# Norms summed by token, the queries' rotation packed, and the gated-attention stage's filling matmuls moved one unit earlier

## The chip, the cores and the metric

One core of a Trainium2 chip runs the whole program. The metric is the device time of one execution in microseconds, the median of the runs shown. The engines are named as in the profile: PE is TensorE, DVE is VectorE, ACT is ScalarE, POOL is GpSimd, SP is SyncE.

## The reference, cut to what matters

A transformer block (multi-head latent attention "MLA", gated linear attention "GLA", a merge, a convolutional feed-forward) is followed by four layers of another kind. Only the first block's token mixer is touched. All is float32, 512 latent tokens and 256 context tokens, 768 together.

```
q = heads(rms_norm(q_c, q_norm_g) @ w_uq)              # 8 heads of 64 + 32 (the 32 are rotated)
k_nope, v = heads(rms_norm(kv_c, kv_norm_g) @ w_ukv)   # 8 heads
p = softmax((q_nope k_nope + rope(q_rope) rope(k_rope)) * MLA_SCALE)
# GLA: 4 heads, 2 directions, chunks of 64 tokens
b_cum = cumsum(g) in the chunk;  kd = k * exp(b_last - b_cum);  ke = k * exp(-b_cum);  qe = q * exp(b_cum)
decay = exp(b_last);  state' = decay * state + kd^T v;  o = mask(qe ke^T) v + qe state
y = rms_norm(o, norm_g) * silu(r)                       # per token and head, over 128 channels
```

## The kernel before

Activations lie channels on partitions, tokens along the free axis. A product in high precision is three fp32r matmuls (high*high, high*low, low*high). `project` makes one output of 128 channels x 512 tokens from k-tiles of a weight panel, `both` makes two outputs (512 latent and 256 context tokens) from the same tiles, `mm` is the line L1576. SP streams weight panels, POOL splits each into `w_hi` and `w_lo`.

Outputs are numbered in one sequence and go to four banks of `acc` in turn: output n may begin only when output n-4 has been taken (`begin_out`, `out_taken`). `both` waits for both of its banks before its first matmul. Every engine works through its own list strictly in order.

The GLA stage is eight units u (head u//2, direction u%2), in the order that `gla_order()` gives. In a unit PE does `turned` (six transposes of the decayed keys kd, L641), `intra` (scores within chunks, L647), `added` (what each chunk adds to the state, L662 and L667), in units 2, 4 and 6 `sum` (L672: the squared outputs of the head before, summed over channels by a matmul with ones, which gives 512 columns on all 128 partitions), `gate` of unit u+2 (L632), a filling projection from `GLA_FILL` (k, q or r of a later head), and the unit's `gla_output` (L684, L690). DVE does `decays(u+1)` (zb, a scan to b_cum, the differences b_last - b_cum into kd, L1244 and L1245), `masked_scores(u)`, `states(u)` (a copy and seven steps, L1292), `decayed_keys(u+1)`, `decayed_queries(u+1)`, and the head's normalisation `head_output` with a reciprocal over 512 columns (L1265). ACT takes outputs from the banks (L868), and makes the exponentials (`key_decays` L934, `sum_decays`, `gate_logs`), squares and roots.

The queries' and keys' low-rank norms are applied by DVE to z_q and z_kv (`low_rank_queries`, `low_rank_keys`) inside units 0 and 1. After the GLA stage PE projects eight outputs for the queries (one a head: 64 plain rows, 32 rotary rows and their 32 partners), then the last head's `sum`, four `both` for the keys, and six value outputs. DVE turns the rotary rows head by head (three operations of 32 partitions each), copies k_rope to the heads, and finishes the last GLA head. Then come 32 attention units of scores, `exps` (L1016), `normalised`, `turn_probs` (L735) and `values` (L752).

Of the kernel before, what the change touches and what calls it, by code (L numbers as in the profile page):

```python
# [70 lines left out]
GH = 4  # L71
# [34 lines left out]
GLA_FILL = [("k", 1, 2), ("q", 1, 1), ("k", 2, 2), ("q", 2, 1), ("k", 3, 2), ("q", 3, 1), ("r", 2, 1), ("r", 3, 1)]  # L106


def gla_order():
    order = [("gate", 0, 2), ("k", 0, 2), ("gate", 1, 2)]  # L110
    for u in range(GLA_STEPS):
        order += [("turned", u, 2), ("intra", u, 1), ("added", u, 1)]
        if u % 2 == 0 and u:
            order.append(("sum", u // 2 - 1, 1))
        if u + 2 < GLA_STEPS:
            order.append(("gate", u + 2, 2))
        order.append(GLA_FILL[u])
    return order
# [5 lines left out]
OUT_V = OUT_KH + HEADS  # L124
# [51 lines left out]
def build(nc, io, names, upto=None, start_x=False):  # L176

    n_panels = io["weights"].shape[0]
    with ExitStack() as whole:
# [163 lines left out]
        with ExitStack() as first:  # L343
# [9 lines left out]
            fb("fill_first", [P, LINE // 8])  # L353
# [5 lines left out]
            with ExitStack() as part:  # L359
# [31 lines left out]
                decay_w = fa("decay_w", [P, GH * P])  # L391
                intra_mask = fa("intra_mask", [P, 2, P])
# [3 lines left out]
                chunk_decay = fa("chunk_decay", [P, 2, NCH])  # L396
            with ExitStack() as part:
# [36 lines left out]
        o_norm = square_sum  # L434

# [25 lines left out]
        gla_d = sem("gla_d")  # L461
# [10 lines left out]
        lr_scaled = sem("lr_scaled")  # L472
        lr_hi = sem("lr_hi")
        lr_lo = sem("lr_lo")
        q_copied = sem("q_copied")
# [73 lines left out]
        def first_block_pe(pe, turn, next_tile, mm, begin_out, project, tile, norm_sum, skip_to_panel):  # L549
# [55 lines left out]
            out = begin_out()  # L605
            for k in range(QL):
                ins = pe.matmul(out[:, :], ones[:, :], low_square[:, T * k:T * k + T], start=(k == 0), stop=(k == QL - 1))
            ins.then_inc(out_made, 1)
            for c0, c1 in ((0, T), (T, TC)):
                out = begin_out()  # L610
                for k in range(KVL):
                    at = QL * T + TC * k
                    ins = pe.matmul(out[:, 0:c1 - c0], ones[:, :], low_square[:, at + c0:at + c1], start=(k == 0),
                                    stop=(k == KVL - 1))
                ins.then_inc(out_made, 1)

            def gla_part(name, i):
# [76 lines left out]
            for name, i, _ in gla_order():  # L694
                gla_part(name, i)
                if (name, i) in [part[:2] for part in GLA_FILL]:
                    gla_output([part[:2] for part in GLA_FILL].index((name, i)))
# [6 lines left out]
            for pair in range(HEADS // 2):  # L704
                both([(kv_hi[:, k, 0:T], kv_lo[:, k, 0:T]) for k in range(KVL)],
                     [(kv_hi[:, k, T:TC], kv_lo[:, k, T:TC]) for k in range(KVL)], T, C,
                     (lambda k: pe.wait_ge(lr_lo, QL + k + 1)) if pair == 0 else None)
            slot, _ = next_tile()
# [99 lines left out]
        def first_block_act(act, feed):  # L808
# [105 lines left out]
            take(OUT_QNORM, square_sum[:, :], func=ACT.Sqrt, bias=col("eps"), scale=1.0 / (QL * P))  # L914
            take(OUT_KVNORM, square[:, 0, :], func=ACT.Sqrt, bias=col("eps"), scale=1.0 / (KVL * P))
            take(OUT_KVNORM + 1, square[:, 1, 0:C], func=ACT.Sqrt, bias=col("eps"), scale=1.0 / (KVL * P), width=C)
# [32 lines left out]
            def head_square(h):  # L949
                act.wait_ge(gla_o, 2 * h + 2)  # L950
                if h == 0:
                    act.wait_ge(lr_scaled, 1)
                act.activation(square[:, h % 2, :], side[:, h % 2, :], ACT.Square).then_inc(gla_sq, 1)

            def head_root(h):
                if h:
                    act.wait_ge(gla_y, h)
                take(OUT_GLA["sum", h], root[:, :], func=ACT.Sqrt, bias=col("eps"), scale=1.0 / P)
                load_exp_ln()

# [8 lines left out]
            gate_logs(1)  # L969
            for u in range(GLA_STEPS):  # L970
# [1504 lines left out]
```

## Time and profile before

| | |
|---|---|
| Median of 3 runs | 3150.24 us (3149.42 to 3150.46) |
| The profiled execution | 3147.42 us, span 3145.4 us |
| PE, POOL, DVE, ACT busy | 97%, 66%, 46%, 22% of the span |
| The chain that ended last | PE 90%, DVE 7%, ACT 2% |

How to read it: PE sets the time, and the rest of the kernel follows it. So the sum of what PE waits, and of what it does at a low granted clock, is what can be won or lost. In windows, PEclk is the mean granted clock as a share of full speed; the two levels are 1.2 and 2.4 GHz. In a timeline, a bracket behind a row is the time for which the engine stood idle ahead of it, and what released it.

### The profile page before, as it was taken

Reading aid. Unit: us, or ns where it says so; the run is one execution under the profiler, and the core shown is the slowest. Engines: PE = TensorE matmul, PEld = TensorE weight load, DVE = VectorE, ACT = ScalarE, POOL = GpSimd, SP = SyncE. Lnnn points to the kernel's source line nnn. Section 1 sums busy time; section 2 is a strip of 40 time slices with the busy share of each in tenths; the row PEclk is TensorE's granted clock in tenths of the full one; section 3 lists DMA queues with packets and bytes.
Section 4 is the critical chain, followed back from the end, with each engine's and each line's share of the span. In section 5 each row is a group of like instructions: output and inputs, shape, how many; then the busy total and the mean of one; then the engine's idle time right before and its main releaser. Section 6 shows DMA issues by size and latency. Waiting matters only on the chain.

```text
span 3145.4 us, 38638 instructions
## 1 busy us (share of the span) xinstructions
PE 3038.9 (97%) x13632; PEld 2471.6 (79%) x13632; DVE 1431.6 (46%) x1871; ACT 681.5 (22%) x1187; POOL 2066.3 (66%) x2056
## 2 busy tenths in 40 slices
PE   5889999999999999999999999999999999999998
PEld 3767668778887788888888888888888887888886
DVE  7877852276456664222325322255422246542222
ACT  3244651111002542111122111100211115421110
POOL 4622217666666677777767777777777776777774
PEclk8989999999999999999999999999999999999999
DMA  6611112222222232232322222222222322332221
GB/s 257 246 41 37 34 54 94 94 81 99 96 97 91 94 102 99 94 100 94 107 87 90 98 94 100 94 97 97 94 100 94 100 94 94 101 100 95 97 97 67
DMA packets 86026, 306.73 MB, mean 98 GB/s; under 512 B 9552, under 2 KB 10064, under 8 KB 85648
## 3 DMA queue, kind: packets, MB, share of 16 engines
q1 hardware_dynamic: 82512, 297.73, 28.0%
q10 hardware_dynamic: 3392, 7.28, 0.7%
q8 instruction: 88, 1.44, 0.2%
q14 instruction: 34, 0.28, 0.0%
HBM read 302.87 MB, written 2.10 MB: 97 GB/s over the span
## 4 chain that ended last, share of the span: by engine, by line
PE 90%; DVE 7%; ACT 2%; issue 1%; SPq 1%; DMA 1%; DVEq 0%; ACTq 0%
PE acc L1576 85%; PE acc L725 1%; DVE rec_rec_x L1999 1%; PE side L752 1%; DVE ada_more L1152 1%; DMA xc<-in_ctx 1%; SPq L531 1%; PE side L735 0%; PE side L1576 0%; PE acc L647 0%; PE stat L1639 0%; DVE n_scaled L1129 0%; PE acc L632 0%; DVE rec_rec_x L1997 0%; DVE att_stat L1347 0%
## 5 line engine op out<-in xcount | busy, mean ns | idle before, releaser
L1538 POOL TENSOR_TENSOR w_lo<-w_raw,w_hi 128x512 fp32r<-128x512 f32 x513 | 671.8, 1310 | 1011.2 <-PE acc L1576 982.9
L1576 PE MATMUL acc<-h_hi,w_hi 128*128 128x512 f32 x2224 | 876.2, 394 | 28.7 <-ACT gq L868 11.6
L1576 PE MATMUL acc<-h_lo,w_hi 128*128 128x512 f32 x2224 | 868.5, 391 | 0.0
L1576 PE MATMUL acc<-h_hi,w_lo 128*128 128x512 f32 x2224 | 868.4, 390 | 0.0
L1539 POOL TENSOR_TENSOR w_lo<-w_raw,w_hi 128x512 fp32r<-128x512 f32 x513 | 709.4, 1383 | 0.0
L1576 PEld LDWEIGHTS acc<-h_hi,w_hi 128*128 128x128 f32 x2224 | 418.9, 188 | 130.2 <-issue 16.8
L1576 PEld LDWEIGHTS acc<-h_lo,w_hi 128*128 128x128 f32 x2224 | 419.5, 189 | 85.5 <-issue 1.9
L1576 PEld LDWEIGHTS acc<-h_hi,w_lo 128*128 128x128 f32 x2224 | 419.4, 189 | 85.2
L1527 POOL TENSOR_SCALAR w_hi<-w_raw 128x512 fp32r<-128x512 f32 x513 | 403.7, 787 | 37.1 <-DMA w_raw<-in_weights 37.1
L1968 DVE TENSOR_TENSOR x<-acc,x 128x512 f32 (+1 forms) x160 | 110.7, 692 | 661.8 <-PE acc L1576 661.7
L1576 PE MATMUL acc<-mlp_hid_hi,w_hi 128*128 128x512 f32 x1024 | 398.3, 389 | 0.0
L1576 PE MATMUL acc<-mlp_hid_lo,w_hi 128*128 128x512 f32 x1024 | 398.3, 389 | 0.0
L1576 PE MATMUL acc<-mlp_hid_hi,w_lo 128*128 128x512 f32 x1024 | 398.3, 389 | 0.0
L1528 POOL TENSOR_SCALAR w_hi<-w_raw 128x512 fp32r<-128x512 f32 x513 | 338.5, 660 | 0.0
L1896 ACT ACTIVATE mlp_hidden<-mlp_relu 128x512 f32<-128x512 f32 x128 | 81.1, 633 | 880.5 <-DVE mlp_relu L2198 880.5
L1975 DVE TENSOR_TENSOR mlp_hid_lo<-mlp_hidden,mlp_hid_hi 128x512 f32 (+1 forms) x128 | 172.3, 1346 | 177.3 <-ACT mlp_hid_hi L1897 177.3
L1576 PEld LDWEIGHTS acc<-mlp_hid_lo,w_hi 128*128 128x128 f32 x1024 | 192.2, 188 | 40.0
L1576 PEld LDWEIGHTS acc<-mlp_hid_hi,w_hi 128*128 128x128 f32 x1024 | 192.2, 188 | 39.9
L1576 PEld LDWEIGHTS acc<-mlp_hid_hi,w_lo 128*128 128x128 f32 x1024 | 192.2, 188 | 39.8
L2198 DVE SCALAR_TENSOR_TENSOR mlp_relu<-acc,norms 128x512 f32<-128x512 f32 x128 | 88.5, 692 | 255.1 <-PE acc L1576 254.5
L1758 ACT ACTIVATE side<-x 128x512 f32<-128x512 f32 x64 | 38.6, 603 | 454.6 <-DVE x L1968 454.6
L1424 DVE SCALAR_TENSOR_TENSOR ff_conv<-acc,table,ff_conv 128x441 f32<-128x441 f32 (+2 forms) x176 | 122.4, 695 | 6.3
(347 smaller groups left out, 3543.4 us busy)
## 6 DMA issues: line engine op xcount, KB each, us to landing
w_raw<-in_weights SPq DMA_DIRECT2D x513, 512.0 KB, 3.3
ada<-in_ada SPq DMA_DIRECT2D x36, 512.0 KB, 5.7
ada_more<-in_ada SPq DMA_DIRECT2D x10, 512.0 KB, 18.2
x<-in_x ACTq DMA_DIRECT2D x16, 256.0 KB, 6.6
out<-x SPq DMA_DIRECT2D x8, 256.0 KB, 2.2
cvec<-in_cvec ACTq DMA_DIRECT2D x1, 1024.0 KB, 5.8
ada_n<-in_ada SPq DMA_DIRECT2D x2, 512.0 KB, 17.3
xc<-in_ctx SPq DMA_DIRECT2D x1, 1024.0 KB, 16.7
```

Of the source, the lines that this page charges most:

```text
L531: sp.dma_start(ada_slot[slot], io["ada"][m]).then_inc(ada_in[slot], 16)
L1424: ins = dve.scalar_tensor_tensor(out=out, in0=src[:, r0 + r:r1 + r, c0 + c:c1 + c], scalar=col("conv_w", FF1 * tap + j), in1=out, op0=ALU. ...
L1527: pool.tensor_scalar(w_hi[:, slot, 0:half], w_raw[:, slot, 0:half], 1.0, 1.0, ALU.mult, ALU.mult)
L1528: pool.tensor_scalar(w_hi[:, slot, half:], w_raw[:, slot, half:], 1.0, 1.0, ALU.mult, ALU.mult).then_inc(hi_made, 1)
L1538: pool.tensor_tensor(w_lo[:, slot, 0:half], w_raw[:, slot, 0:half], w_hi[:, slot, 0:half].bitcast(F32), ALU.subtract)
L1539: pool.tensor_tensor(w_lo[:, slot, half:], w_raw[:, slot, half:], w_hi[:, slot, half:].bitcast(F32), ALU.subtract).then_inc(panel_made, 1)
L1576: ins = pe.matmul(out, lhs, rhs, start=start, stop=stop, skip_group_check=group)
L1758: act.activation(squares(norm, k), x[:, k, :], ACT.Square).then_inc(squared, 1)
L1896: act.activation(M["hidden"][:, o % 4, :], M["relu"][:, o % 4, :], ACT.Square)
L1968: dve.tensor_tensor(tile, bank(o), tile, ALU.add).then_inc(out_taken[o % BANKS], 1)
L1975: dve.tensor_tensor(lo, whole_, hi.bitcast(F32), ALU.subtract).then_inc(made_sem, 1)
L2198: dve.scalar_tensor_tensor(out=M["relu"][:, o % 4, :], in0=bank(o), scalar=0.0, in1=rstd[:, :], op0=ALU.max, op1=ALU.mult).then_inc(out_ta ...
```

## The change

- `k` of head 1 is projected ahead of unit 0; the fillings of units 0 to 4 are then q1, k2, q2, k3, q3, unit 5 has none, and units 6 and 7 keep r2 and r3.
- The differences on DVE (L1244, L1245) go. `key_decays` on ACT copies the chunks' last sums (two small operations), and makes kd by nine exponentials, eight of 64 columns and one of 256, each with the last sum as its bias.
- Sums of squares go by token: the squares are the stationary operand and one column of ones the moving one, so a sum is one column for each block of 128 tokens. Roots and reciprocals are of 4 to 10 columns. A new part `spread` gives a head's factor back to all partitions: ACT makes a diagonal (four copies of the identity scaled by a factor), PE multiplies it by ones, DVE reads the result from the bank in `head_output`. `spread` of a head stands one unit behind its `sum`. `keys` does the same for z_kv (six copies, two matmuls).
- The queries' low-rank factor is not applied to z_q: it goes into the scale of the softmax (`score_scale`, a column operand of `exps` and of the negated maximum), and the channel gain q_norm into `zq_hi` and `zq_lo`.
- The queries' outputs are packed: outputs 0 to 3 hold the rotary rows and partners of four heads each, outputs 4 to 7 the plain rows of two heads each. DVE turns four heads in three operations of 128 partitions, ACT and DVE copy the result to the heads. `rope_q` (512 KB) is loaded by a DMA on ACT's queue behind unit 7.

```diff
-GLA_FILL = [("k", 1, 2), ("q", 1, 1), ("k", 2, 2), ("q", 2, 1), ("k", 3, 2), ("q", 3, 1), ("r", 2, 1), ("r", 3, 1)]
+GLA_FILL = [("q", 1, 1), ("k", 2, 2), ("q", 2, 1), ("k", 3, 2), ("q", 3, 1), None, ("r", 2, 1), ("r", 3, 1)]
-    order = [("gate", 0, 2), ("k", 0, 2), ("gate", 1, 2)]
+    order = [("gate", 0, 2), ("k", 0, 2), ("gate", 1, 2), ("k", 1, 2)]
...
+        if u % 2 == 1 and u > 1:
+            order.append(("spread", u // 2 - 1, 1))
+        if u == GLA_STEPS - 1:
+            order.append(("keys", 0, 2))
...
                 if name == "sum":
-                    pe.matmul(out[:, :], ones[:, :], square[:, i % 2, :], start=True, stop=True).then_inc(out_made, 1)
+                    for b in range(4):
+                        ins = pe.matmul(out[:, b:b + 1], square[:, i % 2, P * b:P * b + P], ones[:, 0:1], start=True, stop=True)
+                    ins.then_inc(out_made, 1)
+                if name == "spread":
+                    pe.wait_ge(head_diag, i + 1)
+                    out = begin_out()
+                    pe.matmul(out[:, :], ones[:, :], square[:, i % 2, :], start=True, stop=True).then_inc(out_made, 1)
...
             def key_decays(u):
-                act.wait_ge(gla_d, u + 1)
-                act.activation(kd[:, :], kd[:, :], ACT.Exp, scale=1.0 / GATE_NORM).then_inc(gla_ed, 1)
+                act.wait_ge(gla_b, u + 1)
+                act.activation(sums_[:, 0:NCH], b_cum[:, last], ACT.Copy, scale=1.0 / GATE_NORM)
+                link(act.activation(sums_[:, NCH:NCH + 1], b_cum[:, end:end + 1], ACT.Copy, scale=1.0 / GATE_NORM))
+                for n in range(NCH + 1):
+                    cols = slice(CHUNK * n, CHUNK * n + CHUNK) if n < NCH else slice(T, TC)
+                    ins = act.activation(kd[:, cols], b_cum[:, cols], ACT.Exp, scale=-1.0 / GATE_NORM, bias=sums_[:, n:n + 1])
+                ins.then_inc(gla_ed, 1)
...
+            def head_diagonal(h):
+                act.wait_ge(head_inverse, h + 1)
+                for b in range(4):
+                    ins = act.activation(square[:, h % 2, P * b:P * b + P], identity[:, :], ACT.Copy, scale=head_rstd[:, 1, b:b + 1])
+                ins.then_inc(head_diag, 1)
+            def key_diagonal():
+                act.wait_ge(low_inverse, 1)
+                for b in range(KB):
+                    ins = act.activation(key_spread[:, P * b:P * b + P], identity[:, :], ACT.Copy, scale=low_rstd[:, 4 + b:5 + b])
+                ins.then_inc(key_diag, 1)
...
-                gla_take(*GLA_FILL[u][:2])
+                if GLA_FILL[u]:
+                    gla_take(*GLA_FILL[u][:2])
+                if d == 0 and h:
+                    head_diagonal(h - 1)
+                if u == GLA_STEPS - 2:
+                    key_diagonal()
+                    for k in range(QL):
+                        act.activation(zq_hi[k], z_q[:, k, :], ACT.Copy, scale=col("q_norm", k)).then_inc(lr_hi, 1)
...
+            head_diagonal(GH - 1)
             for tb in range(KB):
                 take(OUT_V + tb, v_mla[:, tb, :])
...
-                    act.activation(prob[:, u % 2, c0:c1], bank(o + i)[:, 0:c1 - c0], ACT.Exp, scale=MLA_SCALE,
+                    act.activation(prob[:, u % 2, c0:c1], bank(o + i)[:, 0:c1 - c0], ACT.Exp, scale=score_scale[:, 0, qb:qb + 1],
...
             def head_output(h):
-                wait_taken(dve, OUT_GLA["sum", h])
-                link(dve.reciprocal(root[:, :], root[:, :]))
...
+                o = OUT_GLA["spread", h]
+                take(dve.scalar_tensor_tensor(out=o_norm[:, :], in0=gr[:, h % 2, :], scalar=col("gla_norm"),
+                                              in1=bank(o), op0=ALU.mult, op1=ALU.mult), o)
+                own(dve.tensor_tensor(o_norm[:, :], side[:, h % 2, :], o_norm[:, :], ALU.mult), gla_y, h + 1)
...
-                dve.tensor_scalar(kd[:, T:TC], b_cum[:, T:TC], b_cum[:, end:end + 1], -1.0, ALU.subtract, ALU.mult)
-                own(dve.tensor_tensor(chunks(kd[:, 0:T]), chunks(b_cum[:, 0:T])[:, :, last_of[d]].to_broadcast([P, NCH, CHUNK]),
-                                      chunks(b_cum[:, 0:T]), ALU.subtract), gla_d, u + 1)
...
                 if u + 1 < GLA_STEPS:
                     decayed_keys(u + 1)
                     decayed_queries(u + 1)
+                if d == 0 and h:
+                    head_inverses(h - 1)
+                if d == 1 and h:
                     head_output(h - 1)
```

The order of PE at the end of `added` in unit 4 of before, where head 1's sum (`norms,ones`), the gates (`glow,decay_w`) and the filling k of head 3 (`h_hi,w_hi`) follow:

```order
L667 MATMUL side<-v_tok,kd_tok 128x128
L667 MATMUL stat<-v_tok,kd_tok 128x128
L672 MATMUL acc<-norms,ones 128x512 [waits out_taken0,gla_sq]
L632 MATMUL acc<-glow,decay_w 128x512 [waits out_taken1]
L632 MATMUL acc<-glow,decay_w 128x256 [waits out_taken2]
L1576 MATMUL acc<-h_hi,w_hi 128x512 [waits panel_made,out_taken0,out_taken3]
L1576 MATMUL acc<-h_lo,w_hi 128x512
```

And of the change at the end of `added` in unit 3, where the same k of head 3 now follows head 0's spread (`norms,ones`) and the gates:

```order
L686 MATMUL stat<-v_tok,kd_tok 128x128
L686 MATMUL side<-v_tok,kd_tok 128x128
L697 MATMUL acc<-norms,ones 128x512 [waits out_taken2,head_diag]
L651 MATMUL acc<-glow,decay_w 128x512 [waits out_taken3]
L651 MATMUL acc<-glow,decay_w 128x256 [waits out_taken0]
L1649 MATMUL acc<-h_hi,w_hi 128x512 [waits panel_made,out_taken2,out_taken1]
L1649 MATMUL acc<-h_lo,w_hi 128x512
```

The filling has moved a unit ahead, and the output four ahead of its second bank is now the spread and no longer the sum.

The order of DVE in unit 4 of before, from the keys of unit 5 (kd) and queries (`ada`, ke) on to the normalisation of head 1:

```order
L1253 TENSOR_TENSOR kd<-kd,gk 128x768 [waits out_taken0,gla_ed,out_taken3,gla_s]
L1259 TENSOR_TENSOR ada<-ada,gq 128x512 [waits out_taken3,gla_e,gla_kd]
L1260 TENSOR_TENSOR ke<-ke,gk 128x512 [waits dve_chain]
L1265 RECIPROCAL norms<-norms 128x512 [waits out_taken0,gla_qk]
L1268 SCALAR_TENSOR_TENSOR norms<-side,table,norms 128x512 [waits gla_o,out_taken1,dve_chain]
L1270 TENSOR_TENSOR norms<-norms,gr 128x512 [waits dve_chain]
L1232 SCALAR_TENSOR_TENSOR zb<-acc,ln 128x512 [waits gla_ln,gla_y]
```

And of the change in unit 3, from the keys of unit 4 on; `norms<-gr,table,acc` is the operation that reads the spread's bank:

```order
L1309 TENSOR_TENSOR kd<-kd,gk 128x768 [waits out_taken1,gla_ed,out_taken0,gla_s]
L1315 TENSOR_TENSOR qe<-qe,gq 128x512 [waits out_taken1,gla_e,gla_kd]
L1316 TENSOR_TENSOR ke<-ke,gk 128x512 [waits dve_chain]
L1332 SCALAR_TENSOR_TENSOR norms<-gr,table,acc 128x512 [waits out_made,out_taken0,gla_qk]
L1334 TENSOR_TENSOR norms<-side,norms 128x512 [waits out_taken2]
L1295 SCALAR_TENSOR_TENSOR zb<-acc,ln 128x512 [waits gla_ln,gla_y]
L1297 SCALAR_TENSOR_TENSOR zb<-acc,ln 128x256 [waits out_taken3]
```

The reciprocal is gone from the row, and the operation that empties the spread's bank stands behind the multiplications for the next unit.

The order of ACT in unit 6 of the change, from head 2's root on; `gr` is the filling r2, `norms<-identity` are the two diagonals, `hc_hi` and `hc_lo` are zq_hi, `kd_tok` are the takes of unit 7's `turned`:

```order
L901 ACT_TABLE_LOAD
L901 ACTIVATE head_rstd<-acc,table 128x4 [waits out_made]
L844 ACT_TABLE_LOAD
L901 ACT_TABLE_LOAD [waits out_made]
L901 ACTIVATE gr<-acc 128x512 [waits gla_y]
L1004 ACTIVATE norms<-identity,head_rstd 128x128 [waits head_inverse]
L1004 ACTIVATE norms<-identity,head_rstd 128x128 x3
L1010 ACTIVATE norms<-identity,low_rstd 128x128 [waits low_inverse]
L1010 ACTIVATE norms<-identity,low_rstd 128x128 x5
L1044 ACTIVATE hc_hi<-x,table 128x512
L1044 ACTIVATE hc_lo<-x,table 128x512 x2
L901 ACTIVATE kd_tok<-acc 128x512 [waits out_made]
L901 ACTIVATE kd_tok<-acc 128x256 [waits out_made]
```

Ten copies have come in between the take of r2 and the takes of unit 7's transposes.

## Rows read from the trace of the kernel before

**Rows 1.** Windows (start:end, length, busy of each engine with count, PEclk = granted clock).

```profile
335.00:345.00 10.00, 9.17 (x43) 7.81 (x44) 9.79 (x14) 5.90 (x11) 4.75 (x4) 0.83 0.17 52
401.79:403.74 1.95, 1.95 (x12) 1.33 (x11) 1.00 (x2) 1.75 (x5) 0.00 (x0) 1.00 0.00 0
...
500.00:600.00 100.00, 100.00 (x443) 82.81 (x442) 24.87 (x30) 11.58 (x19) 74.27 (x76) 1.00 0.29 95
```

**Rows 2.** Windows, from the transposes to the end of added in four units.

```profile
178.75:186.38 7.63, 5.63 (x32) 4.92 (x32) 6.14 (x9) 4.25 (x9) 0.00 (x0) 0.56 0.00 0
201.66:206.45 4.79, 4.79 (x32) 4.44 (x33) 4.00 (x6) 2.54 (x6) 0.00 (x0) 0.64 0.00 0
216.15:227.05 10.90, 5.50 (x34) 4.69 (x33) 9.99 (x11) 3.15 (x7) 0.00 (x0) 0.69 0.00 0
273.42:276.73 3.31, 3.31 (x34) 3.01 (x33) 1.93 (x4) 2.26 (x6) 0.00 (x0) 1.00 0.00 0
```

**Rows 3.** Timeline of PE (start, us, operation, [idle before <-releaser]), GLA stage.

```profile
178.75 1.54 PE L641 MATMUL acc<-identity,kd 128*128 128x128 f32 x6 [1.19 <-DVE kd L1253]
...
182.28 2.05 PE L647 MATMUL acc<-qe,ke 128*128 128x128 f32 x8 [2.00 <-DVE zb L1232]
...
201.66 0.85 PE L641 MATMUL acc<-identity,kd 128*128 128x128 f32 x6 [2.47 <-DVE zb L1232]
...
222.15 0.69 PE L641 MATMUL acc<-identity,kd 128*128 128x128 f32 x2 [5.40 <-DVE zb L1232]
...
255.01 0.44 PE L641 MATMUL acc<-identity,kd 128*128 128x128 f32 x2 [0.68 <-DVE zb L1232]
```

**Rows 4.** Timeline of PE through one unit.

```profile
258.15 1.12 PE L672 MATMUL acc<-norms,ones 128*128 128x512 f32 x2
...
259.20 1.55 PE L632 MATMUL acc<-glow,decay_w 17*128 17x512 f32 x4
...
262.31 0.47 PE L1576 MATMUL acc<-h_hi,w_hi 128*128 128x512 f32 x1 [1.55 <-issue]
...
270.80 1.05 PE L684 MATMUL side<-a_t,v_tok 128*128 128x128 f32 x8
```

**Rows 5.** Timeline of PE from the projections of the queries to the first scores.

```profile
313.60 0.47 PE L1576 MATMUL acc<-hc_hi,w_hi 128*128 128x512 f32 x1 [1.70 <-DVE hc_lo L1321]
...
335.83 0.76 PE L1576 MATMUL acc<-kv_hi,w_hi 128*128 128x512 f32 x1 [3.20 <-issue]
...
354.18 2.74 PE L725 MATMUL acc<-k_t,q_t 96*128 96x512 f32 x8
```

**Rows 6.** Timeline of DVE in the GLA stage.

```profile
234.32 3.35 DVE L1265 RECIPROCAL norms<-norms 128x512 f32<-128x512 f32 x1
...
242.47 0.69 DVE L1245 TENSOR_TENSOR kd<-b_cum 128x512 f32<-128x512 f32 x1
...
261.96 0.96 DVE L1253 TENSOR_TENSOR kd<-kd,gk 128x768 f32<-128x768 f32 x1
...
279.22 0.35 DVE L1292 SCALAR_TENSOR_TENSOR state<-state,chunk_decay,side 128x128 f32<-128x128 f32 x1
```

**Rows 7.** Timeline of ACT, two pairs of successive rows.

```profile
42.62 0.80 ACT L854 ACTIVATE n_full<-n_scaled,mod,gain 128x512 f32<-128x512 f32 x1
43.32 0.80 ACT L855 ACTIVATE h_hi<-n_scaled,mod,gain 128x512 fp32r<-128x512 f32 x1
...
297.54 1.28 ACT L868 ACT_TABLE_LOAD   x1 [1.32 <-PE acc L1576]
298.83 0.60 ACT L868 ACTIVATE gr<-acc 128x512 f32<-128x512 f32 x1
```

**Rows 8.** Groups of ACT by form (count | busy, mean ns | idle before).

```profile
L934 ACT ACTIVATE kd<-kd 128x768 f32<-128x768 f32 x8 | 6.7, 844 | 13.1 <-DVE kd L1245 13.1
...
L1016 ACT ACTIVATE prob<-acc,att_stat 128x512 f32<-128x512 f32 x32 | 22.1, 691 | 2.0 <-DVE att_stat L1348 2.0
```

**Rows 9.** Timeline of PE, eight one-column matmuls.

```profile
1580.32 1.05 PE L1686 MATMUL side<-ones,norms 1*128 1x1 f32 x8
```

More of the change, by code:

```diff
@@ L391, in build @@
                 decay_w = fa("decay_w", [P, GH * P])
+                with nc.sbuf_tensor("rope_q", [P, 2, T], F32) as rope_q:
+                    pass
                 intra_mask = fa("intra_mask", [P, 2, P])
@@ L950, in head_square @@
                 act.wait_ge(gla_o, 2 * h + 2)
-                if h == 0:
-                    act.wait_ge(lr_scaled, 1)
+                if h >= 2:
+                    wait_made(act, OUT_GLA["spread", h - 2])
                 act.activation(square[:, h % 2, :], side[:, h % 2, :], ACT.Square).then_inc(gla_sq, 1)
             def head_root(h):
-                if h:
-                    act.wait_ge(gla_y, h)
-                take(OUT_GLA["sum", h], root[:, :], func=ACT.Sqrt, bias=col("eps"), scale=1.0 / P)
+                take(OUT_GLA["sum", h], head_rstd[:, 0, :], func=ACT.Sqrt, bias=col("eps"), scale=1.0 / P, width=4)
                 load_exp_ln()
+            def head_diagonal(h):
[8 more added lines that the diff above has]
+                ins.then_inc(key_diag, 1)
             def head_output_high(h):
@@ L993, in first_block_act @@
             act.wait_ge(gla_b, GLA_STEPS)
+            wait_taken(act, OUT_GLA["keys", 0])
+            wait_taken(act, OUT_GLA["keys", 0] + 1)
             for k in range(KVL):
                 act.activation(kv_hi[:, k, :], z_kv[:, k, :], ACT.Copy).then_inc(lr_hi, 1)
-            for h in range(HEADS):
-                wait_made(act, OUT_QH + h)
-                act.activation(q_t[0:64, h, :], bank(OUT_QH + h)[0:64, :], ACT.Copy).then_inc(q_copied, 1)
+            for half in range(2):
+                for pair in (2 * half, 2 * half + 1):
+                    o = OUT_QH + 4 + pair
+                    wait_made(act, o)
+                    act.activation(q_t[0:64, 2 * pair, :], bank(o)[0:64, :], ACT.Copy)
+                    act.activation(q_t[0:64, 2 * pair + 1, :], bank(o)[64:P, :], ACT.Copy).then_inc(out_taken[o % BANKS], 1)
+                if half == 0:
+                    act.wait_ge(q_turned, 1)
+                    for j in range(4):
+                        act.activation(q_t[64:96, j, :], q_rope[0][32 * j:32 * j + 32, :], ACT.Copy)
             head_root(GH - 1)
@@ L1297, in states, with queries_low @@
                         own(ins, gla_s, u + 1)
+            def queries_low():
+                for k in range(QL):
+                    dve.wait_ge(lr_hi, k + 1)
+                    own(dve.scalar_tensor_tensor(out=zq_lo[k], in0=z_q[:, k, :], scalar=col("q_norm", k), in1=zq_hi[k].bitcast(F32),
+                                                 op0=ALU.mult, op1=ALU.subtract), lr_lo, k + 1)
+            low_inverses()
             decays(0)
```

165 lines of the change are left out of this document (91 added, 74 removed).

## The prediction

> **What bounds the kernel now.** I read the page first: PE's share of the span is the largest (the table above), and a window of 100 us behind the attention shows it busy for all of them, with POOL, which splits the weights, at 74 [rows 1]. So PE's own list sets the time, and the change touches only the stretch from the GLA stage to the end of the attention. Next the timeline of PE, for every idle of over 0.5 us from the token sums (160.7) to the first scores (354.18) [rows 3, 4, 5]. In the GLA stage PE waits 1.19 and 2.00 us in unit 0 (for the decayed keys, then for a bank that DVE's zb empties), 2.47 in unit 1, 5.40 in unit 2, 0.68 in unit 4 and as much in unit 6 [rows 3], and 1.55 at the filling k3 in unit 4 [rows 4], where `both` wants the bank of head 1's sum and ACT is at the two table loads around its root. All this is 14.0 us. Behind the long waits the clock is low: from the transposes to the end of `added` PE takes 3.31 us at full clock, and 7.63, 4.79 and 10.90 us in units 0, 1 and 2, at mean clocks of 0.56, 0.64 and 0.69 of 2.4 GHz [rows 2], that is partly at 1.2 GHz. Less the waits inside them (2.00 and 5.40; the first row begins after the 1.19) and less 3.31 each, 2.3, 1.5 and 2.2 us were lost to the clock, 6.0 together. Behind the stage PE waits 1.70 us for the queries' low parts and 3.20 for banks that DVE's head-by-head rotation holds [rows 5], and the clock is at a mean of 0.83 behind that [rows 1].
>
> **GLA stage, what goes.** The waits of units 0 to 2 exist because DVE is late: it spends 3.35 us in each reciprocal over 512 columns [rows 6], two of them and a shorter one in units 0 and 1 before it empties the gates' banks, and 0.69 for the longer of the two differences in each unit [rows 6]. These go, and the k filling ahead of unit 0 (8.5 us, 262.31 to 270.80 [rows 4]) covers the first chain. Walking the new lists with these durations, DVE and ACT are ready before PE in units 0, 1 and 2: what remains there is 0.2 us. I take all of it off: 14.0 + 6.0 = **20.0 us**.
>
> **What PE gets to do in addition.** The fillings only move. Three spreads in the stage cost 1.05 us each (258.15 to 259.20 [rows 4]), the keys' two 1.05 + 0.55 by columns. A one-column matmul is nearest to the eight that take 1.05 us with the last one's latency [rows 9], about 0.11 a pass. A float32 matmul is two passes, as the 512-column sum shows by its x2, so a head's sum is 8 passes, 0.9 instead of 1.05. The three token sums are 48 passes, 5.3 us, as long as the seven matmuls were. Together **+4.3 us**.
>
> **New wait 1, k3 in unit 3.** `both` needs the bank of `spread` 0, and DVE empties it behind its multiplications for unit 4. From the end of `added` (time 0) DVE's eight states last to 2.8 (276.73 [rows 2] to 279.22 + 0.35 [rows 6]), keys and two products take 0.96 + 2 x 0.7 with hand-over 2.45 [rows 6], the read of the bank 0.8: 6.0. PE has spread and gates, 1.05 + 1.5 (259.20 to 262.31 less 1.55 [rows 4]): 2.5. Wait 3.5 us. It lies between the 2.47 and the 5.40 that a low clock followed, so I add 1.5: **5.0 us**. Nothing further is late by it: POOL has made the panel long before, and ACT has its sums and logs done.
>
> **New wait 2, unit 5 to 6.** Unit 5 has no filling. PE comes to the second half of `turned` 6 at 2.5 + 2.6 (270.80 to 273.42 [rows 4, 2]) + 0.5 = 5.6 and finds the spread's bank taken at 6.0 or just after, then `intra` 6 wants a bank of gate 7, which DVE empties after the second product of `head_output` and one zb, at 7.5. On ACT the copy og_hi of that head and a square stand ahead of the takes. 0.5 + 1.15 + 0.25 = **1.9 us**.
>
> **New wait 3, `added` in unit 7.** It needs unit 7's transposes in SBUF, and ACT reaches those takes only behind r2. From the end of r2 ACT loads the Silu table and takes r2, 1.28 + 0.5 [rows 7], makes ten copies of 128 columns with a scale from a column, three zq_hi of 512 with one, and two takes (0.9). A 512-column ACTIVATE takes 0.60 plain [rows 7], 0.69 with one column operand [rows 8], 0.80 with two [rows 7], and its successor starts 0.1 before its end (42.62 to 43.32 [rows 7]). By columns (0.844 for 768, 0.60 for 512 [rows 8, 7]) 128 give 0.33 to 0.38, start to start 0.25. Sum 1.78 + 2.5 + 3 x 0.6 + 0.9 = 7.0. PE has the output (2.6) and transposes and scores (1.6): 4.2. Wait 2.8, and 1.5 of low clock: **4.3 us**. The bounds are 0.15 and 0.35 a copy, a wait of 1.8 to 3.8. For the table there is a rule to weigh. The rows show the load at 297.54 for 1.28 us and the take at 298.83 [rows 7], so nothing follows the load. The Trainium skill ("ScalarE: Activation LUTs", What ACT_TABLE_LOAD costs) counts 1.38 us of drain behind each load; by it this wait would be 4.2 instead of 2.8. The trace does not show that drain. The same page prices an ACTIVATE of 64 columns with a pointer bias at 0.24 us start to start. I take 0.23 from the rows, so the nine exponentials and two copies are 2.6 us against 0.84 [rows 8], and on ACT alone: DVE wants kd only behind its states, over 1 us later.
>
> GLA stage: 20.0 - 4.3 - 0.2 - 5.0 - 1.9 - 4.3 = **4.3 us gained**.
>
> **From the last GLA output to the scores.** Before: 311.90 (313.60 - 1.70) to 354.18, 42.3 us [rows 5]. After, at 0.226 us a matmul (100 us, 443 [rows 1]): 72 for the queries 16.3, small sum 0.9, four key pairs 8.5 (24 of each width, as k [rows 4]), spread 1.05, 36 for the values 8.1: 34.8. The low parts are ready, and DVE's six packed operations empty the banks ahead of PE. But ACT now does more in a row: plain rows, four copies of rotary rows, two table loads and a root, the keys' takes at 2 us a pair, then the last diagonal. PE waits 0.5 for the root's bank, 1.1 at the third pair (ACT is done with the first 6.7 us after the queries' end), and 3.1 at the spread (diagonal done at 13.9, PE there at 10.9), with 1.3 of low clock. 34.8 + 4.7 + 1.3 = 40.8. **1.5 us gained**.
>
> **Attention.** `exps` gets its scale from a column: +0.1 on each of two ACTIVATEs [rows 7, 8], 0.2 us a unit. PE sets the pace in units with `values` and hides it. The first four units and every fourth after have none; in such a one of 1.95 us ACT is busy for 1.75 [rows 1], so 0.2 more fills it. I charge it on 10 of the 32 units, the first four and most of the seven others: **-2.0 us**. Bounds: nothing, and 32 x 0.2 = 6.4.
>
> **Sum.** 4.3 + 1.5 - 2.0 = 3.8 us. The profiled execution took 3147.42, so 3143.6. It lies 2.8 below the median of the runs shown; on that scale 3150.24 - 3.8 = **3146.4 us**. From here the shift passes through to the end, since PE is the bound. A measurement of this kernel tells 0.2% (6.3 us) from no change, so this is no measurable change.
>
> **Rivals.**
> 1. *Faster.* The three long new waits may be followed by no low clock (4.3 us less), as none followed the 1.55 and 1.70 [rows 4, 5], and the attention may hide the scale (2.0). Then 3.8 + 6.3 = 10.1 gained, 3140.1. For it: the clock does not fall behind every wait. Against: it fell behind 2.47 and 3.20.
> 2. *Slower.* ACT becomes the attention's pace. Its price decides: at 0.2 us on all 32 units the sum is 3.8 + 2.0 - 6.4 = -0.6, 3150.8; over 0.2% slower it needs 0.38 a unit, when the longer exponential also delays DVE's sum of the row parts and PE's turn in each unit: 12.2, 3156.6. Against it: ACT idles between units with values.
> 3. *The clock falls in the token sums.* PE streams one column a pass there for 5.3 us. The one row of that kind [rows 9] is 1 us long and tells nothing. If k0 begins at 1.2 GHz as unit 0 did, 2.3 us are lost, perhaps again at a small sum: 3148.7 to 3150.
> 4. *The fillings do not help*, that is, the waits of units 0 to 2 stay in another form, since a chain through ACT (takes, 2.6 us of keys' decays, sums, logs) replaces DVE's. Half of the 20.0 would stay: 3156. The walk gives ACT 21 us in two units of 31, so I hold it unlikely.
>
> **Chances.** The forecast (a gain of 0 to 6) with rival 3: 0.52; rival 1 and what lies between: 0.35; rivals 2 and 4 beyond 6.3: 0.08; small losses otherwise 0.05. So faster 0.35, same 0.56, slower 0.09. The range holds rival 1 whole and of the slow side what a low clock and a full charge in the attention make together (-2.9): 3140 to 3153.
>
> **What would show it.** No PE wait of over 0.5 us in units 0 to 2; PE idle 3.5 us at the first matmul of k3 (released by the spread's read on DVE), about 3 at `added` of unit 7 (ACT's kd_tok) and at the last spread (ACT's copies), each with a clock below 1 behind it; `exps` at 0.79 us instead of 0.69, and attention units without values longer by 0.2. Wrong if the 64-column exponentials cost over 0.4 each, if DVE's products slow down beside POOL (then the wait at k3 is 5 to 6), or if the clock stays low where I have it full.

## The result: 0.41% slower, and the profile after

The changed kernel takes 3161.45 us (median of 6 runs, 3160.24 to 3163.69), the kernel before 3149.83 beside it (6 runs): a ratio of 1.0041, 95% interval 1.0031 to 1.0051. That is 11.6 us more, where a gain of 3.8 was forecast, and outside the range. The profiled execution took 3160.99 us, with a span of 3158.9.

The waits first. These are the rows of the changed kernel's PE timeline with an idle of 0.5 us or more from the token sums to the first attention units, and the first scores; they answer to [rows 3 to 5].

```profile
244.86 0.77 PE L1649 MATMUL acc<-h_hi,w_hi 128*128 128x512 f32 x1 [3.55 <-issue]
282.95 1.67 PE L666 MATMUL acc<-qe,ke 128*128 128x128 f32 x8 [1.10 <-DVE zb L1295]
301.36 1.20 PE L681 MATMUL acc<-v_tok,kd_tok 128*128 128x128 f32 x4 [3.39 <-ACT kd_tok L901]
336.97 0.47 PE L1649 MATMUL acc<-kv_hi,w_hi 128*128 128x512 f32 x1 [0.52 <-ACT head_rstd L901]
340.27 0.47 PE L1649 MATMUL acc<-kv_hi,w_hi 128*128 128x512 f32 x1 [0.97 <-ACT k_t L1071]
347.84 1.74 PE L697 MATMUL acc<-norms,ones 128*128 128x512 f32 x2 [3.13 <-ACT norms L1004]
358.80 2.74 PE L758 MATMUL acc<-k_t,q_t 96*128 96x512 f32 x8
363.11 1.56 PE L758 MATMUL acc<-k_t,q_t 96*128 96x512 f32 x4 [1.56 <-ACT prob L1084]
```

Units 0 to 2 have no wait left, and each new wait stands where it was forecast, within 0.8 us of its length: 3.55 us at k3 (forecast 3.5), 1.10 ahead of `intra` 6 (1.9), 3.39 at `added` 7 (2.8), 0.52, 0.97 and 3.13 behind the stage (0.5, 1.1 and 3.1). The 1.56 at the second scores is not new (1.41 in the kernel before). Windows of the same kernel: from the transposes to the end of `added` in units 0 to 2, then gate 4 and the filling q2 behind head 0's `sum`, then behind the waits (start:end, length, PE busy, granted clock, DMA share, GB/s):

```profile
190.63:194.15 3.52, 3.51 (x35) 1.00 0.00 0
203.84:207.16 3.32, 3.32 (x35) 1.00 0.02 5
219.78:223.14 3.36, 3.36 (x35) 1.00 0.00 0
224.12:232.76 8.64, 8.64 (x29) 0.80 0.17 61
244.86:255.33 10.47, 10.47 (x48) 0.79 0.15 52
282.00:286.00 4.00, 3.05 (x18) 0.67 0.00 0
301.36:306.00 4.64, 4.64 (x20) 0.50 0.00 0
347.84:352.00 4.16, 4.16 (x9) 0.59 0.01 4
```

These parts of units 0 to 2 run at the full 2.4 GHz, in 3.3 to 3.5 us each instead of 7.63, 4.79 and 10.90 [rows 2]. But the clock is low behind the four longer new waits (it stays at 1.00 behind the 0.52 and the 0.97), and for the whole 4.64 us behind the one at `added` 7 it is 1.2 GHz. It is low behind head 0's `sum` too, where PE had waited for nothing. So the structure is as forecast, and yet the stage ends at 316.15 us, where 307.6 was forecast (311.90 less the 4.3 to be gained in it). The first part of what is missing stands ahead of unit 0, in the timeline of PE at the token sums:

```profile
160.44 7.07 PE L628 MATMUL acc<-ones,low_square 128*128 128x1 f32 x48
167.44 2.92 PE L651 MATMUL acc<-glow,decay_w 17*128 17x512 f32 x4
170.29 0.79 PE L1649 MATMUL acc<-h_hi,w_hi 128*128 128x512 f32 x1
```

The 48 passes take 7.07 us, not 5.3; gate 0 takes 2.9 us where a gate takes 1.55 at full clock [rows 4]; and k0, from 170.29 on, takes 10.35 us where k3 took 8.5.

The second part is not in the changed code at all. Compared by the start of the same instruction, the changed kernel is 4.6 us later at the first scores (354.18 and 358.80), 5.2 at the last scores (437.78 and 442.99), 7.9 where the merge ends (623.06 and 630.98), 10.5 at the end of the feed-forward (998.07 and 1008.60), and there is no new wait between. The spans differ by 13.5; the last 3.0 are taken up at the end of this document. Windows of 40 us inside the feed-forward's down projection and of 100 us inside its up projection, kernel before:

```profile
661.00:761.00 100.00, 100.00 (x443) 1.00 0.29 97
950.00:990.00 40.00, 40.00 (x178) 1.00 0.28 92
```

and the changed kernel:

```profile
661.00:761.00 100.00, 100.00 (x443) 1.00 0.30 100
950.00:990.00 40.00, 40.00 (x173) 1.00 0.26 92
```

PE never idles and the granted clock is full in all four, but in the down projection it gets through 173 matmuls instead of 178. Start to start they take 0.2333 us instead of 0.2267 (means of the 512-column matmuls over 20 us of the timeline). The slow stretches are 120 to 150, 320 to 360, 460 to 640, 820 to 860 and 930 to 1010 us; everywhere else the two kernels agree. The first one begins before any changed instruction has run.

### The profile page after: what moved, and what is told of

It reads as the page before. It is cut to its first block, busy times and chain, and to the rows that moved or that the text cites. A ratio compares the mean times of both kernels' runs of the same rounds, so it can differ in the third digit from the quotient of the medians.

```text
span 3158.9 us, 38762 instructions
## 1 busy us (share of the span) xinstructions
PE 3058.0 (97%) x13702; PEld 2484.4 (79%) x13702; DVE 1397.3 (44%) x1838; ACT 707.5 (22%) x1293; POOL 2068.6 (65%) x2056
## 4 chain that ended last, share of the span: by engine, by line
PE 91%; DVE 5%; ACT 2%; SPq 1%; issue 1%; DMA 1%; ACTq 0%; DVEq 0%
PE acc L1649 85%; PE acc L758 1%; DVE rec_rec_x L2072 1%; PE side L785 1%; DVE ada_more L1218 1%; SPq L549 1%; DMA xc<-in_ctx 1%; PE side L768 0%; PE acc L651 0%; PE side L1649 0%; PE side L721 0%; PE stat L1712 0%; DVE n_scaled L1195 0%; DVE att_stat L1420 0%; DVE rec_rec_x L2070 0%
## 5 line engine op out<-in xcount | busy, mean ns | idle before, releaser
L1649 PE MATMUL acc<-h_hi,w_hi 128*128 128x512 f32 x2224 | 877.4, 395 | 32.5 <-ACT gq L901 11.6
```

Source lines behind the costliest of these rows:

```text
L1649: ins = pe.matmul(out, lhs, rhs, start=start, stop=stop, skip_group_check=group)
```

## The experiments

Theories: A, one-column passes lower the clock. B, the slow cadence hangs on the place of an instruction in PE's list. C (rival to B), it comes from the change's own work or timing. D, each new wait costs its length and low clock behind it, and order alone can remove it. Theories E to G come up on the way. The last column is the median less that of the kernel before on the same chip (3148.86 us for the first four, 3148.37 for the next four, 3150.39 for the last four).

| Run | us | ratio, 95% interval | us to before |
|---|---|---|---|
| e1_wide_sums | 3155.16 | 1.0020 [1.0011, 1.0029] | +6.3 |
| e2_before_pad | 3149.10 | 1.0002 [0.9993, 1.0011] | +0.2 |
| e3_after_pad | 3161.05 | 1.0042 [1.0028, 1.0055] | +12.2 |
| e4_order | 3145.09 | 0.9987 [0.9978, 0.9996] | -3.8 |
| e6_aligned | 3154.57 | 1.0019 [1.0010, 1.0028] | +6.2 |
| e7_before_32 | 3156.50 | 1.0029 [1.0017, 1.0040] | +8.1 |
| e8_before_64 | 3152.92 | 1.0014 [1.0005, 1.0023] | +4.6 |
| e9_all | 3131.35 | 0.9946 [0.9933, 0.9960] | -17.0 |
| e10_weights_32 | 3224.53 | 1.0237 [1.0223, 1.0251] | +74.1 |
| e11_moving_32 | 3192.46 | 1.0132 [1.0116, 1.0147] | +42.1 |
| e12_old_fill | 3174.80 | 1.0069 [1.0055, 1.0082] | +24.4 |
| e13_scale | 3158.97 | 1.0026 [1.0016, 1.0036] | +8.6 |

**The sums by tokens, 128 columns a pass.**

```diff
-pe.matmul(out[:, b:b + 1], low_square[...], ones[:, 0:1], ...)
+pe.matmul(out[:, P * b:P * b + P], low_square[...], ones[:, :], ...)
```

> The changed kernel with one thing different: the sums by tokens stream all 128 columns of the ones through each pass instead of one column (each result stands 128 times, and ScalarE reads every 128th). The number of passes and weight loads stays the same. Theory A (the one-column passes lower the granted clock: the 48 passes took 7.07 us at a clock of 0.74, then gate 0 2.78 us at 0.50 and k0 10.35 us at 0.81): the sums take 5 to 5.5 us, gate 0 about 1.5 and k0 8.6, and the whole is 4 to 6 us faster than the changed kernel, 3156 to 3157. Rival (the clock falls there because weights are swapped in every pass, or for a reason outside the sums): the clock stays at 0.5 in gate 0, and the time 3161 or more. Theory B (the slow cadence of 0.2333 us in code that the change leaves alone hangs on where the instructions stand in TensorE's list): the same stretches as in the changed kernel are slow (580 to 640, 820 to 860, 920 to 1010 us), since no instruction is added.

It was 5.3 us faster than the changed kernel (+6.3 against +11.6). Timeline of PE in this run, and its windows over gate 0 and k0 and over gate 4 and q2 behind head 0's `sum`:

```profile
161.50 5.52 PE L628 MATMUL acc<-ones,low_square 128*128 128x128 f32 x48
166.95 1.55 PE L651 MATMUL acc<-glow,decay_w 17*128 17x512 f32 x4
```

```profile
170.00:181.00 11.00, 11.00 (x59) 1.00 0.14 49
220.63:227.69 7.06, 7.06 (x30) 1.00 0.05 12
```

and windows of the changed kernel, from the end of the sums through gate 0, and the same one:

```profile
165.00:170.00 5.00, 5.00 (x16) 0.50 0.13 53
170.00:181.00 11.00, 11.00 (x50) 0.81 0.15 48
```

A is shown: 128 times the columns make the sums 1.55 us shorter, since the clock stays at 2.4 GHz in them, in gate 0 and in k0. The edit widens the heads' sums too, and gate 4 and q2 take 7.06 us at full clock instead of 8.64 at 0.80. The clock does not fall at every one-column sum: behind head 1's it stays full in the changed kernel (from 261.31 us). At the full clock a pass costs 5.52 / 48 = 0.115 us with 128 columns. In the changed kernel the passes of one column start 0.112 us apart as long as the clock is full (160.46 to 163.81), and 0.213 behind that. So the columns are free here: the weight load, the same in both, is what is left to set the pace of a pass. The Trainium skill (TensorE: Matmul & The Clock Gate, LDWEIGHTS) gives a load's time in ns as its columns divided by 1.2, an estimate of 0.107 us for 128; the trace agrees to 0.01.

**Place in the list.** The same 35 (29) harmless products ahead of everything, in the kernel before and in the changed one:

```diff
+for _ in range(35):
+    pe.matmul(side[:, 0, 0:1], ones[:, :], ones[:, 0:1], start=True, stop=True)
```

> The kernel before, with 35 more one-column float32 products (70 passes, as many as the change adds) at the very start, where TensorE is idle until 21 us; nothing else is changed. Theory B (the cadence hangs on the place in TensorE's list): matmuls of the first block take 0.2333 us start to start in the same stretches as in the changed kernel, and the time goes up by about 6 us, to 3156. Rival C (the cadence comes from the change's own work, or from its timing): every stretch stays at 0.2267, and the time is 3149.5 to 3151.

> The changed kernel with 29 more one-column float32 products (58 passes) at the very start, where TensorE is idle; nothing else is changed. Theory B: the slow stretches move or vanish, and the time changes by 1 to 6 us in one direction or the other. Rival C: they stay at 580 to 640, 820 to 860 and 920 to 1010 us, and the time stays at 3161 within 1 us.

Neither moved: +0.2 and +12.2, with the slow stretches absent in the one and in place in the other (0.2333 us at 600 to 620 us, with the products ahead and without). B is refuted: 70 and 58 more passes ahead of everything change nothing. C stood, but the stretch at 120 us spoke against it: whatever slows PE there is present before the change does anything. What is different from the first instruction is where tiles lie. The allocator's byte addresses in a partition, of the two kernels:

```
tile          before           changed
h_hi          32896            32896         moving tile of most matmuls, both 0 over a multiple of 64
low_rstd      -                132352        new, 40 bytes, takes 64
og_hi, ff_hi  132480           132512        0 and 32 over a multiple of 64
hc_hi         174464           174496        as above, and so for all of hc, zq, kv, om, og, mg, ff
```

`fill_first` is a tensor that nothing uses; it only keeps the addresses behind it. The change made it shorter by the sizes of the three new tensors, but the allocator gives each of them whole units of 32 bytes. So all that lies behind moved by 32 bytes, and these are the tiles of the slow stretches. That is theory E.

**Back to the old addresses, and the old kernel at the new ones.**

```diff
-fb("fill_first", [P, LINE // 8 - (QL + 1 + KB) - 16])        # e6, in the changed kernel
-fb("fill_first", [P, LINE // 8])                             # in the kernel before
+fb("fill_first", [P, LINE // 8 + 8])                         # e7: 32 bytes; e8: + 16, 64 bytes
```

> The changed kernel with one line less: the filler tensor behind the three new small ones is gone. In the changed kernel the new tensors and the filler take 32 bytes more per partition than the old filler, so every tile of the first block that stands behind them lies 32 bytes further, at addresses that are 32 over a multiple of 64; without the filler they lie again where they lay before. No instruction changes. Theory E (a matmul whose moving or stationary tile lies off a multiple of 64 bytes takes 0.2333 us instead of 0.2267): all tiles concerned are those of the slow stretches (hc, zq, kv, om, og, mg, ff, some 1,020 matmuls of 512 columns at 6.7 ns), every stretch goes back to 0.2267, and the time is 6 to 8 us less, 3153.5 to 3155.5. Rival C (the change's timing makes the cadence): 3161, same stretches.

> The kernel before with its filler longer by 32 bytes per partition, so that every tile of the first block behind it lies 32 bytes further; no instruction changes. Theory E: the same stretches as in the changed kernel take 0.2333 us a matmul, and the time is 6 to 8 us more, 3155 to 3157. Rival C: no change, 3149.

> The kernel before with its filler longer by 64 bytes per partition. Theory E (64 bytes is the grain): no change, 3148 to 3150, 0.2267 throughout. Rival (the grain is 128 bytes or more): as with 32 bytes, 3155 or more.

Same window as above, in turn e6, e7 and e8:

```profile
950.00:990.00 40.00, 40.00 (x178) 1.00 0.30 95
```

```profile
950.00:990.00 40.00, 40.00 (x173) 1.00 0.29 93
```

```profile
950.00:990.00 40.00, 40.00 (x176) 1.00 0.30 104
```

E is shown from both sides: without an instruction changed, the repair takes 5.4 us off (+6.2 against +11.6; 6 to 8 were expected) and the shift puts 8.1 on the kernel before. Some 1,090 fp32r matmuls of 512 columns read shifted tiles (528 of ff, 192 of mg, 192 of om and og, 132 of zq, kv and the values, 48 of hc); at 6.7 ns they make 7.3, between the two. C is refuted. The third expectation failed: a shift of 64 bytes costs too, 4.6 us, at 0.2289 us a matmul. The old addresses are 128 over a multiple of 256; with 32 bytes more a matmul takes 6.7 ns more, with 64 it takes 2.2 ns more. The slow cadence does not come from 64-byte lines alone. It is also not in every product: the old sums over low-rank squares are plain float32 and not fp32r, their moving tile lies behind the filler, and the timelines of the kernel before and of e7 show them equally long.

```profile
160.68 2.74 PE L607 MATMUL acc<-low_square,ones 128*128 128x512 f32 x6
```

```profile
161.40 2.74 PE L607 MATMUL acc<-low_square,ones 128*128 128x512 f32 x6
```

**Which operand.** Only the weights' tiles, then only h_hi and h_lo, 32 bytes off, in the kernel before:

```diff
+sb("ahead", [P, 8])        # ahead of w_raw (e10) or of h_hi (e11)
...
+sb("behind", [P, 56])      # behind w_lo (e10) or h_lo (e11)
```

> The kernel before, with the weights' tiles (w_raw, w_hi, w_lo) alone 32 bytes off a multiple of 64; what stands ahead of them is where it was, what stands behind them 256 bytes further. No instruction changes. They are the stationary tiles of some 12,000 matmuls of 512 columns and the moving ones of some 370. Theory E1 (any tile off a multiple of 64 bytes costs 6.7 ns a matmul): 0.2333 us throughout, some 80 us more, 3228. Theory E2 (only the moving tile counts, which is read for 512 columns): 0.2267 for nearly all, +2.5 us, 3151.

> The kernel before, with h_hi and h_lo alone 32 bytes off a multiple of 64, and what stands behind them 256 bytes further. They are the moving tiles of some 6,600 matmuls of 512 columns and the stationary ones of some 300. Theories E1 and E2: 0.2333 us for these, 44 us more, 3192. Theory E3 (only the stationary tile counts): +2 us, 3150.

Windows of e10:

```profile
661.00:761.00 100.00, 100.00 (x430) 1.00 0.28 95
950.00:990.00 40.00, 40.00 (x173) 1.00 0.29 100
```

and of e11:

```profile
661.00:761.00 100.00, 100.00 (x431) 1.00 0.26 91
950.00:990.00 40.00, 40.00 (x178) 1.00 0.30 101
```

E1 holds. With the weights off, every stretch is slow (430 instead of 443, 173 instead of 178), and the kernel takes 74.1 us more; with h off, of these two windows only the up projection's is, whose moving tile it is, and the down projection, which reads ff, keeps its 178. Either operand alone costs the whole step. In every slow run one operand moved and its partner did not. So the runs do not tell whether the address of a tile counts or the difference between the addresses of the two: none moves both by the same 32 bytes. The Trainium skill (SBUF — State Buffer, Specifications) gives SBUF cachelines of 16 bytes. Our reading, that a shift by two whole lines should then cost nothing, does not hold here; the measurement decides.

**Order.**

```diff
 states(u)
+if d == 1 and h:
+    head_gated(h - 1)           # DVE: first product of head_output, which empties spread's bank
...
+if u == 3:
+    key_diagonal()              # ACT, during k3; it was in unit 6, ahead of unit 7's takes
+if u == GLA_STEPS - 1:          # zq_hi: behind unit 7's takes; it was in unit 6
...
+if h == 2:                      # PE: the last head's sum behind the second rotary output,
+    gla_part("sum", GH - 1)     # and its root, inverse and diagonal there on ACT and DVE
```

> The changed kernel with its new waits taken out by order alone: VectorE empties the bank of a spread right behind the states; ScalarE makes the keys' diagonal during k3, and the queries' high parts behind the takes of unit 7; the last head's sum stands behind the second rotary output, so that root, inverse and diagonal are made while ScalarE and VectorE idle, and 5 of the 8 rotary copies of the keys go ahead as well. Theory D (each new wait costs its length and about 1.5 us of low clock behind it): the waits of 3.55, 3.39, 0.52, 0.97 and 3.13 us go, 11.5 us, and 3 to 4.5 us of low clock with them: 3145.5 to 3147.5. Rival (a wait costs only itself, as the clock falls later instead): 3150. Rival (the work that is moved meets other waits): a wait of over 1 us in units 3 to 7 or at the keys, and 3152 or more.

3145.09: 15.4 us less than the changed kernel (-3.8 against +11.6), as much as D forecast. What PE still waits in this run:

```profile
243.19 0.47 PE L1665 MATMUL acc<-h_hi,w_hi 128*128 128x512 f32 x1 [1.11 <-issue]
280.85 1.77 PE L672 MATMUL acc<-qe,ke 128*128 128x128 f32 x8 [1.57 <-DVE zb L1304]
329.23 0.47 PE L1665 MATMUL acc<-kv_hi,w_hi 128*128 128x512 f32 x1 [1.39 <-ACT q_t L1070]
348.79 1.56 PE L765 MATMUL acc<-k_t,q_t 96*128 96x512 f32 x4 [1.01 <-ACT prob L1093]
```

The seven waits of the changed kernel were 14.2 us, these four are 5.1. So 9.1 of the 15.4 us were idle time; D had 11.5, and took k3 and the keys to be free of waits, where 1.11 and 1.39 stand. The other 6.3 should be the low clock behind the waits; D had 3 to 4.5. The sum came right because the two misses cancel. Windows from `added` 7 to the end of the keys' spread, and from the last spread to the first scores, in the changed kernel:

```profile
301.36:307.91 6.55, 6.55 (x24) 0.55 0.00 0
347.84:358.80 10.96, 10.96 (x38) 0.84 0.15 49
```

and in this run:

```profile
295.78:299.54 3.76, 3.76 (x25) 1.00 0.00 0
335.79:345.04 9.25, 9.25 (x40) 1.00 0.19 58
```

These two are 2.8 and 1.7 us of the 6.3, and k3 (10.47 against 10.03 us) is 0.4; the remaining 1.4 are not located, and lie within the spread of the runs.

**The old fillings**, with the rest of the change kept:

```diff
-order = [("gate", 0, 2), ("k", 0, 2), ("gate", 1, 2), ("k", 1, 2)]
+order = [("gate", 0, 2), ("k", 0, 2), ("gate", 1, 2)]        # and the old GLA_FILL
```

> The changed kernel with the old fillings: k1 in unit 0 instead of ahead of it, and each later one a unit later. The rest of the change stays (no differences, short reciprocals, sums by tokens). Theory F (it is k1 ahead of unit 0 that covers the first chain): waits of 1 to 4 us come back in units 0 and 1 with low clock behind them, 5 to 9 us; k3 moves to unit 4, where its bank is free, and its wait of 3.55 with 1.5 of low clock goes; in all 3161 to 3166. Rival G (VectorE's short work alone removes the early waits, and the fillings' place costs only the wait at k3): 3155 to 3158.

Slower than any expectation, +24.4: 12.8 us more than the changed kernel. Its five runs took from 3168.8 to 3175.2 us. Timeline of this run, in unit 0 and at the fillings k2 and k3, and two windows over unit 0:

```profile
185.66 1.54 PE L660 MATMUL acc<-identity,kd 128*128 128x128 f32 x6 [3.10 <-DVE kd L1308]
189.19 2.05 PE L666 MATMUL acc<-qe,ke 128*128 128x128 f32 x8 [1.99 <-DVE zb L1294]
...
231.67 0.76 PE L1648 MATMUL acc<-h_hi,w_hi 128*128 128x512 f32 x1 [2.12 <-issue]
...
268.79 0.77 PE L1648 MATMUL acc<-h_hi,w_hi 128*128 128x512 f32 x1 [2.13 <-issue]
```

```profile
185.66:194.02 8.36, 6.37 (x32) 0.50 0.01 2
194.02:207.74 13.72, 13.72 (x54) 0.71 0.11 38
```

F is right for unit 0: without k1 ahead PE waits 5.1 us there, at 1.2 GHz, and the clock is low far into k1. It is wrong elsewhere. The wait at k3 does not go but stands twice, with 2.1 us at k2 and at k3. And ahead of the transposes of units 1 and 2, where the kernel before waits 2.47 and 5.40 us [rows 3], PE waits for nothing although the fillings are the old ones. A part of this is PE's own delay: from unit 0's transposes to unit 1's it takes 24.7 us here (185.66 to 210.36), and in the kernel before 20.4 without the wait, 4.3 less. The 5.40 is more than that. So G is right for at least a part of unit 2's wait, which goes by the rest of the change and not by the fillings; for unit 1 the run does not tell, and for unit 0 and for the time G is refuted.

**The scale of the exponentials** as a number:

```diff
-scale=score_scale[:, 0, qb:qb + 1]
+scale=MLA_SCALE
```

> The changed kernel with the exponentials' scale and the maximum's factor as numbers in the instruction instead of columns; this leaves the queries' norm out of the scores. The forecast charged 2.0 us for the columns in the attention, the traces of the two kernels differ by 0.7 between its first and last scores. By the forecast 3159.5, by the traces 3160.8; a gain of over 3 would mean that ScalarE sets the pace in the attention.

The instructions of `exps` (count: duration in ns, min/median/max), in the changed kernel and in this run:

```profile
L1084 ACT ACTIVATE prob<-acc,att_stat,score_scale x64: 554/688/819, 362.2 to 448.1; 128x512 f32<-128x512 f32 x32, 128x256 f32<-128x256 f32 x32
```

```profile
L1084 ACT ACTIVATE prob<-acc,att_stat x64: 465/588/694, 363.3 to 450.1; 128x512 f32<-128x512 f32 x32, 128x256 f32<-128x256 f32 x32
```

Each is 0.1 us longer with the column, as forecast. What that costs is not settled by the times: +8.6 against +11.6 looks like 3.0, but the intervals overlap. From first to last scores the profiled execution took 85.3 us, against 84.2 in the changed kernel and 83.6 in the kernel before. But its attention alone of the three has a stretch at 1.2 GHz, as this window of it shows:

```profile
365.90:369.30 3.40, 3.40 (x10) 0.50 0.00 0
```

Less half of these 3.4 us (an estimate) it is 83.6, as in the kernel before. By that the column costs 0.6 us.

**All three repairs together.** The edits of e1, e4 and e6.

> The changed kernel with all three repairs: the order of the fourth experiment, the sums by tokens with 128 columns, and the tiles back on multiples of 64 bytes. If the three gains add up (16.4 in the fourth run, 6.3 in the first, 7 by theory E): 3131 to 3133. Rival (they overlap, since each shift of phase moves low clock elsewhere): 3134 to 3139.

3131.35 us, 0.54% faster than the kernel before: -17.0 against +11.6 is 28.6 us, and the three alone gave 5.3 + 15.4 + 5.4 = 26.1. They add up within the noise. What PE waits in this run:

```profile
237.21 0.47 PE L1664 MATMUL acc<-h_hi,w_hi 128*128 128x512 f32 x1 [1.11 <-issue]
274.97 1.13 PE L671 MATMUL acc<-qe,ke 128*128 128x128 f32 x8 [1.56 <-DVE zb L1303]
321.69 0.47 PE L1664 MATMUL acc<-kv_hi,w_hi 128*128 128x512 f32 x1 [1.52 <-ACT q_t L1069]
341.08 1.56 PE L764 MATMUL acc<-k_t,q_t 96*128 96x512 f32 x4 [1.01 <-ACT prob L1092]
```

## Why the prediction was wrong, by its steps

The miss is 15.4 us (11.6 lost where 3.8 were to be gained). By the two traces it is 17.3: the GLA stage ends 8.5 us later than forecast (316.15 against 307.6), the part from there to the scores is 1.9 longer, the attention 1.4 shorter, and 8.3 are lost behind it, where the forecast had nothing (5.3 up to the end of the feed-forward, 3.0 behind). Three steps failed, the first three of this list.

- **"From here the shift passes through to the end, since PE is the bound": wrong, 5.4 us** (e6; 8.1 by e7). PE is the bound, and for that reason every matmul's own pace counts. The prediction held that code which the change does not touch keeps its pace, and put the three new tensors at nothing. The filler's line in the full diff was the sign: it is there to keep addresses, and 104 + 24 bytes in four pieces are 160 when each is rounded up.
- **"The three token sums are 48 passes, 5.3 us": wrong, 5.3 us** (e1). The price of a pass was right at the full clock (5.52 for 48). Rival 3 had the mechanism, and priced it at 2.3 for k0, "perhaps again at a small sum". The sums themselves (1.55), gate 0 (1.4) and k0 (1.85) were all hit, 4.8 by the trace, and gate 4 and q2 behind head 0's sum once more (1.6).
- **The new waits: right in place and length, within 0.8 us each; the low clock behind them: wrong, too small.** It was charged at 1.5, 1.5 and 1.3 us, 4.3 in all, and at nothing in unit 6. By the traces it took 2.0 at k3 (10.47 us instead of 8.5), 1.5 in unit 6 (4.18 us for `intra` and `added`, 2.70 in unit 4), 2.8 at `added` 7 and behind it (6.55 against 3.76 in e4) and 1.7 at the last spread (10.96 against 9.25 in e4): 8.0 together, 3.7 more than charged. That is most of the 4.7 us of the miss which the first two steps leave. The rest is within the spread of the runs.
- **Units 0 to 2: right.** No wait, and full clock up to head 0's sum. e12 shows that k1 ahead of unit 0 buys that unit's two waits, and that the rest of the change (VectorE's shorter work, by the walk) takes off at least a part of unit 2's. Rival 4 did not come.
- **Behind the stage: the waits right, the sum not.** The forecast was 40.8 us from the last GLA output to the scores, measured 358.80 - 316.15 = 42.65. 132 matmuls of 512 columns there read shifted tiles (0.9 us), and the clock was 0.59 for 4.16 us behind the last spread. (The prediction also passed over an idle of 0.62 us at 329.27 in the kernel before; its 42.3 was read as a whole, so the sum does not change.)
- **Attention, -2.0: too much by the trace** (84.2 us against 83.6: 0.6), and the trace of e13 agrees; its times do not settle it. Rival 2 did not come.

## What to carry to other kernels

Where PE is the bound, compare the tiles' addresses of the two kernels before believing that untouched code keeps its time; a new small tensor should stand behind the matmul's tiles, or its filler be worked out from rounded sizes. A float32 matmul of one column with a new weight costs as much as one of 128 and may cost the clock behind it. In e4 a wait on PE was worth 1.7 times its length (15.4 us for 9.1), so an order that shifts waits from one place to another should be walked for all engines first, as e4 did.

## What the runs showed of the hardware

- A matmul of 512 columns in fp32r takes 0.2267 us start to start with both tiles 128 over a multiple of 256 bytes, 0.2333 with either tile 32 bytes further, and 0.2289 (a mean over the three kinds of product) with its tile in the first block 64 bytes further, all at a granted clock of 1.00. At 2.4 GHz the step of 6.7 ns is 16 cycles. Plain float32 sums show no such step. Other addresses were not tried, nor both tiles moved alike; whether one is faster than the old ones stays open.
- 48 passes of one column took 7.07 us, with the clock falling to 1.2 GHz in them, 48 of 128 columns 5.52 us at 2.4 GHz.
- Runs of the same program spread over 4 us (the kernel before 3146.93 to 3150.63 in 27 runs) and up to 7 (e10). Two traces differ also by where the clock falls at waits of the later layers, which both kernels have. Behind a wait of 1.91 us at VectorE it is 0.66 in the changed kernel (1095.40 to 1100.40), and 1.00 in the kernel before (1083.20 to 1088.20). Between 1010 and 3130 us the clock is at 1.2 GHz for 17.1 us in the trace of the changed kernel, and for 10.2 in that of the kernel before. At half clock the 6.9 us more are 3.4 us lost (an estimate), about the 3.0 by which the traces part behind the feed-forward.
